# A hybrid encoder layer on one core: earlier token copies, an expert search over two halves, a reordered tail

## What is computed

```
h = rmsnorm(x);  x = x + token_mixers(h, w_in, ...)      # attention + bidirectional SSD, w_out
h = rmsnorm(x)
logits = h @ w_router                                    # (tokens, 16 experts)
aff = softmax(logits, axis=-1)
gate, idx = top_k(aff.T, cap)                            # cap = 128 (sample), 64 (prompt)
xe = h[idx]                                              # rows of each expert
ye = (silu(xe @ w_gate[e]) * (xe @ w_up[e])) @ w_down[e] * gate
x = x.at[idx].add(ye)                                    # scattered back, added
y = rmsnorm(x) * final_g
```

## Time and profile before

| | us |
|---|---|
| three runs | 2047.68, 2048.57, 2053.80 |
| their median | 2048.57 |
| the profiled execution, its time | 2047.24 |
| the profiled execution, its span | 2045.5 |

### The profile page before, as it was taken

The page is one execution under the profiler, slowest core; times in us unless marked ns, Lnnn a source line. Parts: engine busy times, 40 slices in busy tenths (PEclk is TensorE's granted clock), DMA queues, the critical chain, the costliest instruction groups (busy, mean ns, idle before and its releaser), DMA issues. The chain is left out here.

```text
span 2045.5 us, 31641 instructions
## 1 busy us (share of the span) xinstructions
PE 1876.5 (92%) x11560; PEld 1667.7 (82%) x11560; DVE 1520.3 (74%) x2235; ACT 1063.8 (52%) x1531; POOL 511.9 (25%) x384
## 2 busy tenths in 40 slices
PE   5999998998889989887894999999999999999995
PEld 5887876886669987665594999999999999999994
DVE  4335787997867569997676787877777777878785
ACT  3323336885661433266632556565655555555564
POOL 2444433331860123342601001111111100111121
PEclk8999999999999989989996999999999999999997
DMA  5332321000023422210145677777777777777885
GB/s 188 110 113 99 104 74 40 1 1 1 22 80 138 166 93 88 88 42 1 53 146 191 219 249 263 244 269 256 249 240 248 235 250 261 240 269 242 306 283 216
DMA packets 63043, 326.18 MB, mean 159 GB/s; under 512 B 8368, under 2 KB 14640, under 8 KB 32752
## 3 DMA queue, kind: packets, MB, share of 16 engines
q1 hardware_dynamic: 46640, 265.55, 36.9%
q0 software_dynamic: 16320, 59.52, 10.0%
HBM read 288.08 MB, written 35.39 MB: 158 GB/s over the span
## 5 line engine op out<-in xcount | busy, mean ns | idle before, releaser
L2330 PE MATMUL psum<-xT,whi 128*128 128x384 f32 x1024 | 296.0, 361 | 1.2 <-DVE xT L1898 1.2
L2330 PE MATMUL psum<-xT,whi_x 128*128 128x384 f32 x1024 | 293.7, 359 | 0.0
L1923 PE MATMUL psum<-ht_hi,whi 128*128 128x512 f32 (+1 forms) x624 | 240.3, 385 | 32.1 <-POOL wlo L581 13.0
L1832 DVE TENSOR_TENSOR wlo_x<-wraw_x,whi_x 128x2048 fp32r<-128x2048 f32 x96 | 218.3, 2286 | 57.6 <-ACT whi_x L1178 57.6
L2331 PE MATMUL psum<-xT,wlo 128*128 128x192 f32 x1024 | 257.5, 251 | 0.0
L2331 PE MATMUL psum<-xT,wlo_x 128*128 128x192 f32 x1024 | 256.4, 250 | 0.0
L1924 PE MATMUL psum<-ht_lo,whi 128*128 128x512 f32 (+1 forms) x624 | 237.2, 380 | 0.0
L1925 PE MATMUL psum<-ht_hi,wlo 128*128 128x512 f32 (+1 forms) x624 | 237.0, 380 | 0.0
L1832 DVE TENSOR_TENSOR wlo<-wraw,whi 128x2048 fp32r<-128x2048 f32 x94 | 213.4, 2282 | 17.5 <-ACT whi L1178 17.5
L581 POOL TENSOR_TENSOR wlo<-wraw,whi 128x2048 fp32r<-128x2048 f32 x36 | 167.5, 4654 | 231.3 <-ACT whi L801 231.3
L2331 PEld LDWEIGHTS psum<-xT,wlo 128*128 128x128 f32 x1024 | 197.0, 192 | 0.6
(11 more groups left out here) (377 smaller groups left out, 4414.3 us busy)
## 6 DMA issues: line engine op xcount, KB each, us to landing
wraw<-moe_chunks SPq DMA_DIRECT2D x96, 1024.0 KB, 5.3
wraw_x<-moe_chunks SPq DMA_DIRECT2D x96, 1024.0 KB, 6.2
wraw<-w_in_chunks SPq DMA_DIRECT2D x36, 1024.0 KB, 5.0
wraw<-w_out_chunks SPq DMA_DIRECT2D x8, 1024.0 KB, 5.8
xin<-x POOLq DMA_DIRECT2D x12, 512.0 KB, 5.2
acc_scratch<-x POOLq DMA_DIRECT2D x12, 512.0 KB, 3.7
h_scratch<-h POOLq DMA_DIRECT2D x12, 512.0 KB, 4.4
fin<-acc_scratch SPq DMA_DIRECT2D x11, 512.0 KB, 9.4
```

Of the source, the lines that this page charges most:

```text
L1832: tt(moe_lo[i % 4], moe_raw[i % 4].rearrange("p (k n) -> p k n", k=KT), moe_hi[i % 4].bitcast(F32), ALU.subtract).then_inc(w_lo_done, 1)
L1923: mm(out, wh, xh, start=first, stop=False, **kw)
L2330: mm(bank[:, 0:2 * TOK], hi[:, k, cols], xT[:, k, :], start=(k == 0), stop=False)
```

## The change

The change has three parts in one kernel.

**A. Start.** Two semaphores of the constants become one. The wait for `gain` moves into `normed(0)`, ahead of the multiplication. ScalarE makes tile 0's high part before the first weight split and tile 1's right behind it, then the squares of tiles 2 and 3; VectorE makes the low parts around its own split, then `normed(2)` and `normed(3)`. The selectors and memsets come after the low parts of tiles 2 and 3. TensorE turns tiles 2 and 3 together. In block 2 the two `normed` stand ahead of the memsets.

**B. Search.** `affT` becomes 64 partitions x half a sequence: the first half of the tokens on partitions 0 to 15, the second on 32 to 47. Half the transposes (of 64 columns) and one copy fill it. A round searches both halves at once, over half the length, and `chosen` merges the two sorted lists: the second is reversed, the larger of each pair is kept with its index.

**C. Tail.** The tiles are normalised in the order prompt first (8 to 11, then 0 to 7). Expert 14's sample rows then fall into tiles that are loaded after they are added, so only its prompt rows are repaired: one gather, one norm and one scatter of 128 rows go. Six load semaphores take the place of four, and a load waits for the square six tiles back, not four. ScalarE's squares and roots are dealt out anew over the last chunks, `final_stage`'s roots a chunk later. The two semaphores of the adding scatters become one. The wait for the last two scatters moves from GpSimd to the end of SP's program.

```diff
-        aff = at("aff", 80, [P, P])
+        aff = at("aff", 80, [P, 4, 2, 32])
-        affT = at("affT", 120, [NE, 1024])
+        affT = at("affT", 120, [64, 512])
...
             def choose(s, n):
-                L, o_ = SEQS[s][1] * P, 128 * s + 8 * n
+                L, o_ = SEQS[s][1] * P // 2, 128 * s + 8 * n
...
             def chosen(s):
+                own.step(dve.tensor_copy(vb, topv[second, cols][:, ::-1]))
                 own.link(dve.tensor_copy(topf[:, cols], topi[:, cols]))
-                own.link(ts(topf[:, cols], topf[:, cols], float(SEQS[s][0] * P), None, ALU.add))
+                own.step(tt(m, va, vb, ALU.is_ge))
+                own.step(ts(fb, topf[second, cols][:, ::-1], float(SEQS[s][0] * P + SEQS[s][1] * P // 2), None, ALU.add))
+                own.link(ts(fa, fa, float(SEQS[s][0] * P), None, ALU.add))
+                own.step(tt(va, va, vb, ALU.max))
+                own.link(tt(fa, fa, fb, ALU.subtract))
+                own.link(tt(fa, fa, m, ALU.mult))
+                own.link(tt(fa, fa, fb, ALU.add))
...
+                own.step(dve.memset(aff[:, :, :, NE:32], 0.0))
...
-                for q in range(L // 512):
-                    own.step(dve.tensor_copy(affT[:, q * 512:(q + 1) * 512], pb[2 + q][0:NE, :]))
-                own.wait()
+                own.link(dve.tensor_copy(affT[:, 0:L // 2], pb[2][0:64, 0:L // 2]))
...
-                for i in range(nt):
-                    last = pe.transpose(pb[2 + i // 4][0:NE, (i % 4) * P:(i % 4 + 1) * P], aff[:, i * NE:(i + 1) * NE],
-                                        ident)
+                for i in range(nt // 2):
+                    last = pe.transpose(pb[2][0:64, i * P:(i + 1) * P], aff[:, i].rearrange("p h n -> p (h n)"), ident)
...
             rms(1)
+            tokens_hi(0)
             split(0)
+            tokens_hi(1)
+            rms(2)
+            rms(3)
...
                     if b == 0:
-                        tokens_hi(0)
-                        rms(2)
-                        tokens_hi(1)
-                        rms(3)
                         tokens_hi(2)
                         tokens_hi(3)
...
-            dve.wait_ge(gain_in, 16)
             normed(0)
             normed(1)
+            tokens_lo(0)
             split(0)
-
-            own.step(dve.tensor_reduce(head_sel[:, :], ident.rearrange("p (j h) -> p h j", h=4), AX.X, ALU.add))
...
+            tokens_lo(1)
+            normed(2)
+            normed(3)
...
                 for b in blocks:
-                    for j in range(2):
-                        if b == 0:
-                            tokens_lo(j)
-                        if b != 1:
-                            normed(TPB * b + j + 2)
+                    if b == 2:
+                        normed(10)
+                        normed(11)
                     for j in (2, 3):
                         tokens_lo(TPB * b + j)
+                    if b == 0:
+                        selectors()
+                    if b == blocks[0]:
+                        dve.memset(tmp[:, :, :], 0.0).then_inc(tmp_clear, 1)
...
                         turn_tokens(TPB * b + 2)
+                        if b == 0:
+                            turn_tokens(3)
                         column_tile(1, early)
-                        turn_tokens(TPB * b + 3)
+                        if b:
+                            turn_tokens(TPB * b + 3)
...
-                if t >= 4:
-                    sp.wait_ge(fss, squared(t - 4))
-                sp.dma_start(final_tile(t), acc_dram[t * P:(t + 1) * P, :]).then_inc(y_in[t % 4], 16)
+                if n >= 6:
+                    sp.wait_ge(fss, squared(n - 6))
+                sp.dma_start(final_tile(n), acc_dram[final_rows(n), :]).then_inc(y_in[n % 6], 16)
...
-            for j in (8, 9, 10):
-                chunk_split(sp, last, j)
-                for t in ((7, 8), (9,), (10, 11))[j - 8]:
-                    load_final(t)
-            sp.wait_ge(fix_out, 32)
-            for t in range(4, NT):
-                store_final(t)
+            chunk_split(sp, last, 8)
+            for n in range(7, NT):
+                load_final(n)
+            sp.wait_ge(fix_out, 16)
+            for n in range(4, NT):
+                store_final(n)
+            sp.wait_ge(end_out, 32)
...
-            pool.indirect_dma_start(out=fix_s[:, :], out_offset=None, in_=acc_dram, in_offset=rows_at(si_s)
-                                    ).then_inc(fix_in, 16)
...
-            pool.indirect_dma_start(out=y, in_=fix_s[:, :], in_offset=None, out_offset=rows_at(fi_s)
-                                    ).then_inc(fix_out, 16)
...
-            pool.wait_ge(end_out, 32)
...
-                for n in {(LATE, 6): (0,), (LATE, 7): (1,), (LATE, 8): (2, 3), (LATE + 1, 6): (12, 13),
-                          (LATE + 1, 7): (4,)}.get((e, j), ()):
+                for n in {(LATE, 6): (0,), (LATE, 7): (1,), (LATE, 8): (2, 3), (LATE + 1, 6): (12,),
+                          (LATE + 1, 7): (4,), (LATE + 1, 8): (5,)}.get((e, j), ()):
                     final_square(n)
...
-                if (e, j) == (LATE + 1, 8):
+                if (e, j) == (LATE + 1, 9):
                     act.wait_ge(fms, 2)
-                    act.activation(small[:, 6, 0:1], small[:, 5, 0:1], ACT.Sqrt)
                     act.activation(small[0:64, 6, 1:2], small[0:64, 5, 1:2], ACT.Sqrt)
-                    roots(2, small[:, 1, 4:5], small[:, 2, 4:5])
-                    final_square(5)
-                    final_square(6)
-                if (e, j) == (LATE + 1, 9):
-                    final_square(7)
-                    final_square(8)
-                    roots(3, small[:, 1, 5:9], small[:, 2, 5:9])
+                    roots(2, small[:, 1, 4:6], small[:, 2, 4:6])
+                    for n in (6, 7, 8):
+                        final_square(n)
+                    roots(3, small[:, 1, 6:9], small[:, 2, 6:9])
```

More of the change, by code:

```diff
@@ L300, in hybrid_encoder @@
         ys_done, tp_done, yp_done = sem("ys_done"), sem("tp_done"), sem("yp_done")
-        sc_s, sc_p = sem("sc_s"), sem("sc_p")
-        y_in = [sem(f"y_in{i}") for i in range(4)]
+        rows_added = sem("rows_added")
+        y_in = [sem(f"y_in{i}") for i in range(6)]
         fss, fms, frms, fy, y_out = sem("fss"), sem("fms"), sem("frms"), sem("fy"), sem("y_out")
@@ L523, in _ @@
                     sp.wait_ge(scattered, LATE + 1)
-                for t in {5: (0, 1), 6: (2,), 7: (3,)}.get(j, ()):
-                    load_final(t)
+                for n in {5: (0, 1), 6: (2,), 7: (3,)}.get(j, ()):
+                    load_final(n)
             last = NE - 1
@@ L1131, in final_square @@
                 if n < NT:
[L1132 removed]
+                    act.wait_ge(y_in[n % 6], 16 * (n // 6 + 1))
                     src, out = final_tile(n), small[:, 0, n:n + 1]
[L1134 to L1136 removed]
+                elif n == NT:
+                    act.wait_ge(fix_in, 16)
+                    src, out = fix_p[:, :], small[0:64, 4, 1:2]
                 else:
[L1138 removed]
+                    half, i = (n - 13) // 2, (0, 1, 1, 0)[n - 13]
                     cols = slice(half * BLK, (half + 1) * BLK)
@@ L1199, in expert @@
                         if half == 0:
-                            for n in norm_order[3]:
+                            for n in (9, 10, 11):
                                 final_square(n)
                             roots(4, small[:, 1, 9:NT], small[:, 2, 9:NT])
-                        else:
+                            final_square(13)
+                            final_square(14)
+                        else:
+                            final_square(15)
+                            roots(5, small[0:64, 5, 5:6], small[0:64, 6, 5:6])
                             final_square(16)
-                            roots(5, small[0:64, 5, 5:6], small[0:64, 6, 5:6])
-                            final_square(17)
                             roots(6, small[:, 5, 3:4], small[:, 6, 3:4])
@@ L1861, in expert @@
                         half = (j - 9) // 2
-                        for i in (0, 1) if half == 0 else (1, 0):
-                            end_half(e, half, i)
                         if half == 0:
+                            roots_in(3, 6, 9)
+                            final_norm(6)
+                            end_half(e, 0, 0)
+                            end_half(e, 0, 1)
                             final_norm(7)
+                            dve.wait_ge(fss, squared(11))
+                            mean_squares(9, NT)
                             final_norm(8)
-                            dve.wait_ge(fss, squared(11))
+                            roots_in(4, 9, NT)
+                            for n in range(9, NT):
+                                final_norm(n)
+                            dve.wait_ge(fss, squared(14))
                             own.step(ts(small[:, 5, 2:3], small[:, 4, 2:3], 1.0 / D, EPS, ALU.mult, ALU.add))
```

(12 more changed lines are left out.)

141 lines of the change are left out of this document (70 added, 71 removed).

## The result

| | before | changed |
|---|---|---|
| median of the runs, us | 2051.19 (4 runs, 2047.68 to 2054.01) | 2020.43 (4 runs, 2019.86 to 2022.99) |
| profiled execution, us (span) | 2047.24 (2045.5) | 2020.55 (2018.7) |

The ratio is 0.9857, with a 95% interval of 0.9841 to 0.9872: 29 us faster, 26 to 33 (the two medians differ by 30.8). The forecast was 2024.0 with a range of 2016.5 to 2032, and faster with a chance of 0.93. The spans of the two profiled executions differ by 26.8 us, where the sum had 24.0.

What follows compares the result with a forecast made beforehand. Expert loop already full (TensorE 877.39 of 878 us), VectorE pacing the third block; gains sought in TensorE's waits. Terms 6.5 + 1.4 + 5.0 + 5.9 + 2.6 + 2.6 = 24.0 us off profiled 2047.24; taken 2024.0, range 2016.5 to 2032.

Steps and rivals of the forecast that it cites:

- start: First 36 us: TensorE's waits for low parts of token tiles 1 and 3 shrink or go; 6.5 us, ends 4.9 and 6.9.
- first router phase: Router phase ahead of the first search: four transposes and one copy fewer on the path; 1.4 us, ends 0.7 and 1.5.
- search beside block 2: Third input block: shorter search instructions free VectorE, TensorE loses about 5 us instead of 10.3; 5.0 us, ends 0 and 10.3.
- second router phase: TensorE's 10.53 us wait for the second search's last mark shrinks with half-length rounds; 5.9 us, ends 4.9 and 6.3.
- tail order: After the expert loop: last weight split earlier without the sample rows' repair, stores then limit; 2.6 us, ends 1 and 4.1.
- end: After the last scatter: GpSimd drains while SyncE waits for the landing; 2.6 us, or 0 if the drain runs from landing.
- The replay: Start: new order with the old trace's durations; first column tile at 19.1, second half of tile 0 at 28.7 (was 35.27).
- The cover of the selectors: Start: selectors and memsets (2.4 us of VectorE) moved behind tile 3 are cheap while 1.2 us of slack holds.
- the slower rival: Both searches: instruction time goes with elements over all partitions, so 61 us slower, 2109; decides from 1.43 us; chance 0.03.
- The rival of uncovered splits: Block 2 gains 1 us or nothing as GpSimd splits hold VectorE, drain may stay; gain 16.4 to 20; chance 0.21.
- all waits go: Block 2 gains the full 10.3 us and the tail 4.1; 30.8 us in all, so 2017; chance 0.09.
- the gains don't carry: Parts work, but a wait further on eats their gains; less than 6 us is left; chance 0.04.

## Why the prediction was right, term by term

| term | forecast, us | found, us | from |
|---|---|---|---|
| start | 6.5 | 6.1 | TensorE's waits, 8.89 + 1.57 down to 4.34 |
| first router phase | 1.4 | 1.0 | start of block 2's first tile, 7.96 earlier, 6.92 at the transposes ahead of it (727.24, 720.32) |
| search beside block 2 | 5.0 | 7.5 | waits for `wlo` and `stage`, 10.3 to 2.8 |
| second router phase | 5.9 | 5.4 | wait for the mark, 10.53 to 5.13 |
| tail order | 2.6 | 3.3 | last scatter 23.82 earlier, the expert loop 20.53 |
| end | 2.6 | 2.9 | scatter to end, 12.0 to 9.1 |
| sum | 24.0 | 26.2 | 0.6 more as a net of clock and landings: 26.8 |

That the sum is met so closely is in part luck. The found terms are mostly waits, and around them stand pieces of up to 3 us that happen to cancel. Of the start's 6.1 only 5.25 were there at tile 0's second half. The granted clock gave 1.5 at the join of the first two blocks and 2.5 in the third. Then 3.4 was taken between the third block and the second search, 2.6 of it near 1060, where the clock is 0.50 in the changed kernel's profile. None of these pieces was in the prediction.

**The start.** The replay held in what it said is gone and what is late next. The first column tile came at 20.3, not 19.1, because the first token tile landed 1.0 later in this run (7.91 for 6.88): counted from that landing it moved from 17.1 to 12.4 us, 4.7 where I had 4.9. The step that failed here is that the replay took one trace's landings as fixed: as the profiles stand, the second half of tile 0 came 5.25 us earlier, not 6.5. The cover of the selectors held, and was needed. The last of them, a copy of 128x16, ran under GpSimd's second split:

```profile
30.04 4.59 DVE L1314 CAST unit_row<-conv_acc 128x16 fp32r<-128x16 f32 x1
```

It took 4.59 us and ended with the split (29.98, 4.61 long), so the part "2.4 us of VectorE" was really near 7, hidden because TensorE had no wait for VectorE there. The prediction's "at most their 2.4" without the cover was too low.

**First router phase.** The transposes were mis-sized: four of 64 columns took 1.06 us, where I had halved the 1.51 of eight. The second router phase came out 0.5 under its term, which no run takes apart.

**The search.** That length and not partitions sets the price was right to 1 ns, and the slower rival fell with it (it needed 1430 ns). The step that failed is the overlap in block 2, the share of TensorE's 10.3 us that stays. I had put 5.3 there, by a replay and by the second block's 4.4; it was 2.8. I had counted held instructions (8 of 12 splits, and up to 2 more); the dearer multiply-adds are worth one more. What I had not counted is that VectorE, once ahead, absorbs them. Nor had I counted that a wait can cost TensorE more than its length: behind the wait of 4.9 the clock fell, 1.5 us more, so this part is worth about 9 us to TensorE and not 7.5. The second block was a poor witness; its convolutions are twice as long, but no run tests that this is why. The Trainium skill, page "SBUF — State Buffer", section "Who interferes with whom", says that a VectorE instruction with two SBUF inputs contends with a GpSimd instruction that reads SBUF, that issue order decides which of them blocks, and that one with at most one SBUF input outside the two-port modes does not contend. The runs agree: multiply-adds that meet a split take some 5 us and MAX8 stays at 681. The result that I had drawn from it, a term near 1 us, was wrong, since it priced held instructions as if TensorE waited for each.

**The tail** was right in its parts: VectorE's last weight split stands at 1985.36 instead of 2009.97, 24.6 us earlier and so 4.1 ahead of the expert loop's 20.53, as forecast, and the idle 2.1 us of the earlier trace rows are gone:

```profile
L1891 DVE TENSOR_SCALAR small<-small 128x1 f32<-128x1 f32 x1 | 0.1, 146 | 0.0
```

**The end** is shown by two runs: the drain has a length of its own, 8 us, and is bought once, behind GpSimd's last instruction. The Trainium skill's "VectorE: DVE Perf Modes", section "The DRAIN you can't avoid", gives some 12 ns for the drains of a preamble and postamble. This one has a line of the kernel (L89) and takes 8 us on GpSimd, so that figure doesn't price it, and the 21.4 of the prediction fell.

**The sum against the runs.** By the ratio the gain is 29 us and not 24. In the profiles 2.5 of the difference is the third block's waits and about 1 the tail and the end; and the profiled execution that I summed against lay 4 us below the median of the four runs of before. The rival of uncovered splits is refuted as a bound, not as a mechanism. That all waits go came true for these waits of block 2 (0.2 left) once two rounds were moved. That the gains don't carry fell: 20.53 us enter the expert loop, and 23.8 reach the last scatter.

## What to carry to other kernels

A search by rounds costs by the length of a row, so folding the row over idle partitions nearly halves it (1211 to 681 ns an instruction here) at the price of one short merge. When work on an engine is shortened, ask not only what it now collides with but how far ahead the engine gets: collisions cost nothing while an engine is early by more than they hold it. A wait that goes can give back more than its length where the clock fell behind it. And look at what the engine that ends last waits for: a wait put on an engine with a long drain pays the drain after the wait, put elsewhere it pays both at once (2.7 us here).

## What was not expected of the hardware

- A profile of the same kernel can differ by 4.8 us (2018.7 and 2023.5) with equal waits, because the granted clock falls behind a wait of some 3 us in one run and not in the next. A single profiled span can't judge a term below some 5 us; its waits can, and nearly all came again within 0.2 us.
- A copy of 128x16 on VectorE took 4.59 us, the rest of the GpSimd subtraction that had started just before it.
- GpSimd's drain at the end takes 7.9 to 8.3 us behind its last indirect transfer or wait, whether or not that transfer has landed.
